# Sliding attention one unit at a time between the half tiles of a projection, with the gate recurrences beside its last tiles

## What is computed

```python
proj = h @ w_in[l]
q_a, k_a, v_a, q_m, k_m, v_m, o_m, i_m, f_m, g_a, g_m = jnp.split(proj, split_points, axis=-1)
...
y_a = sliding_window_attention(q_a, k_a, v_a, attn_sinks[l]).astype(x.dtype)

qk_m = jax.nn.silu(causal_depthwise_conv(jnp.concatenate([q_m, k_m], axis=-1), conv_w[l], conv_b[l]))
q_m, k_m = jnp.split(qk_m, 2, axis=-1)
i_pre = i_m + b_if[l][:MLSTM_HEADS]
f_pre = f_m + b_if[l][MLSTM_HEADS:]
h_m = mlstm_chunkwise(..., i_pre, f_pre)
y_m = (jax.nn.sigmoid(o_m.astype(jnp.float32)) * head_layer_norm(h_m, mlstm_norm_w[l])).astype(x.dtype)
merged = jax.nn.sigmoid(g_a) * (y_a @ w_branch_attn[l]) + jax.nn.sigmoid(g_m) * (y_m @ w_branch_mlstm[l])
```

## Time and profile before

| | us |
|---|---|
| median of 3 runs | 3319.88 |
| lowest and highest | 3318.41, 3323.91 |
| the profiled execution, its own time | 3337.6 |
| its span in the profile | 3335.7 |
| TensorE busy, share of the span | 3004.1, 90% |
| VectorE busy | 1268.3, 38% |
| ScalarE busy | 1017.8, 31% |
| GpSimd busy | 1001.5, 30% |
| mean granted clock of TensorE, share of full speed | 0.932 |

### The profile page before, as it was taken

The page is one execution under the profiler, slowest core; times in us unless marked ns, Lnnn a source line. Parts: engine busy times, 40 slices in busy tenths (PEclk is TensorE's granted clock), DMA queues, the critical chain, the costliest instruction groups (busy, mean ns, idle before and its releaser), DMA issues. The chain is left out here.

```text
span 3335.7 us, 38189 instructions
## 1 busy us (share of the span) xinstructions
PE 3004.1 (90%) x13920; PEld 2449.9 (73%) x13920; DVE 1268.3 (38%) x1998; ACT 1017.8 (31%) x1820; POOL 1001.5 (30%) x708
## 2 busy tenths in 40 slices
PE   3988966799899999999999788778989999998998
PEld 2876755566678888878888666667877888886877
DVE  6745235211152000001455886652436323333133
ACT  3223223100152000002444556524435212222243
POOL 2000311121263233224552122341035333332454
PEclk8987988899999999999999899885899999998999
DMA  5510200121241111113341122000034111111342
GB/s 189 179 59 0 63 13 0 38 57 38 79 142 57 50 50 44 50 37 120 123 130 45 39 64 88 26 13 1 0 101 139 32 50 48 47 50 56 102 142 92
DMA packets 191476, 221.46 MB, mean 66 GB/s; under 512 B 11145, under 2 KB 140297, under 8 KB 191369
## 3 DMA queue, kind: packets, MB, share of 16 engines
q1 hardware_dynamic: 191368, 220.05, 20.8%
HBM read 199.05 MB, written 20.97 MB: 66 GB/s over the span
## 5 line engine op out<-in xcount | busy, mean ns | idle before, releaser
L132 PE MATMUL psum<-sb_h_hi,sb_w_hi 128*128 128x512 f32 x1792 | 706.4, 394 | 13.8 <-POOL sb_w_lo L1038 9.2
L134 PE MATMUL psum<-sb_h_hi,sb_w_lo 128*128 128x512 f32 x1792 | 699.3, 390 | 0.0
L133 PE MATMUL psum<-sb_h_lo,sb_w_hi 128*128 128x512 f32 x1792 | 699.2, 390 | 0.0
L1424 POOL TENSOR_TENSOR sb_out_lo<-sb_out_raw,sb_out_hi 128x512 fp32r<-128x512 f32 (+1 forms) x180 | 323.3, 1803 | 410.4 <-ACT sb_out_hi L1414 410.3
L1036 POOL TENSOR_SCALAR sb_w_hi<-sb_w_raw 128x1024 fp32r<-128x1024 f32 x112 | 118.2, 1056 | 953.1 <-PE psum L134 676.1
L132 PEld LDWEIGHTS psum<-sb_h_hi,sb_w_hi 128*128 128x128 f32 x1792 | 337.6, 188 | 87.9 <-issue 13.4
L132 PE MATMUL psum<-sb_out_hi,sb_a_hi 128*128 128x512 f32 x960 | 382.3, 398 | 18.7 <-DVE sb_a_lo L1419 10.6
L133 PEld LDWEIGHTS psum<-sb_h_lo,sb_w_hi 128*128 128x128 f32 x1792 | 337.8, 189 | 73.4 <-issue 3.8
L134 PEld LDWEIGHTS psum<-sb_h_hi,sb_w_lo 128*128 128x128 f32 x1792 | 337.5, 188 | 70.5
L133 PE MATMUL psum<-sb_out_lo,sb_a_hi 128*128 128x512 f32 x960 | 378.3, 394 | 0.0
L134 PE MATMUL psum<-sb_out_hi,sb_a_lo 128*128 128x512 f32 x960 | 377.5, 393 | 0.0
(11 more groups left out here) (381 smaller groups left out, 4290.3 us busy)
## 6 DMA issues: line engine op xcount, KB each, us to landing
sb_w_raw<-in_w_up SPq DMA_DIRECT2D x44, 512.0 KB, 3.8
sb_late_w<-in_w_ada SPq DMA_DIRECT2D x32, 512.0 KB, 4.9
sb_w_raw<-in_w_in SPq DMA_DIRECT2D x56, 256.0 KB, 3.0
sb_w_raw<-in_w_in SPq DMA_DIRECT2D x28, 512.0 KB, 5.4
sb_w_raw<-in_w_ffn_gate SPq DMA_DIRECT2D x22, 512.0 KB, 3.8
sb_w_raw<-in_w_ffn_up SPq DMA_DIRECT2D x22, 512.0 KB, 3.9
sb_out_raw<-in_w_ffn_down SPq DMA_DIRECT2D x22, 512.0 KB, 3.6
sb_out_raw<-in_w_ffn_down SPq DMA_DIRECT2D x44, 256.0 KB, 3.0
```

What stands on the lines that cost most here:

```text
L132: nc.tensor.matmul(out, stationary.hi, moving.hi, start=start, stop=False)
L133: nc.tensor.matmul(out, stationary.hi, moving.lo, start=False, stop=False)
L134: return nc.tensor.matmul(out, stationary.lo, moving.hi, start=False, stop=stop)
L1424: self.nc.gpsimd.tensor_tensor(w.lo, raw, w.hi.bitcast(F32), ALU.subtract).then_inc(self.w_lo, 1)
```

## The change

The three blocks become one, which keeps the name `window_phase`. TensorE's stream is a straight list of 24 half tiles, numbered s; a half tile is 24 matmuls. The first 16 of them carry a unit each: the scores of unit s stand before half tile s, the transposes of unit s-1 after three of its eight feature blocks, the product with v of unit s-1 after six. Output rows are turned at odd s. The other engines' lists follow the same numbers. The convolution of a tile is given to VectorE in two parts, two taps in one step and one in the next. The gate work is a class, `Gates`: its inputs are turned in half tile 18, its results in half tile 23, its VectorE part stands at the end of VectorE's list, and its ScalarE parts stand between the sigmoids. The copies of the query block and key window are gone. The loops over tiles and query blocks are written out. Buffers have other places in SBUF, and `yaT` takes the place of `qT`, block by block.

```diff
+        @block.tensor
+        def _(pe):
+            def steps(s, first, last):
+
+                m, hf = s // 2, s % 2
+                if first == 0:
+                    if hf == 0:
+                        pe.wait_ge(split_done, m + 1)
+                    if m >= 2:
+                        if m - 2 < n_qk:
+                            pe.wait_ge(taps_done, m - 1)
+                        else:
+                            pe.wait_ge(o_done, m - 1 - n_qk)
+                for k in range(first, last):
+                    done = multiply(nc, core.ps[:, 2 * (m % 2) + hf, :], w[:, m % 2, k], h.half(k, hf), k == 0, k == KD - 1)
+                if last == KD:
+                    done.then_inc(mm_done, 1)
+
+            def scores(u):
+                n, g = u // 2, u % 2
+                if u:
+                    pe.wait_ge(s_read, u)
...
+            def turn(u):
+                pe.wait_ge(exp_done, 5 * u + 5)
+                if u:
+                    pe.wait_ge(o_read, u)
+                if u >= 2:
+                    pe.wait_ge(ya_out, u // 2)
...
+            def outputs(u):
+                n, g = u // 2, u % 2
+                pe.wait_ge(t_out_act, u + 1)
+                pe.wait_ge(t_out_dve, u + 1)
...
+            for s in range(2 * M):
+                if s < U:
+                    scores(s)
+                if s >= 3 and s % 2 and s <= U + 1:
+                    turn_outputs((s - 3) // 2)
+                steps(s, 0, 3)
+                if 1 <= s <= U:
+                    turn(s - 1)
+                steps(s, 3, 6)
+                if 1 <= s <= U:
+                    outputs(s - 1)
+                if s == U + 2:
+                    pe.wait_ge(ya_out, TB)
+                    gates.turn_in(pe)
+                if s == 2 * M - 1:
+                    gates.turn_out(pe)
+                steps(s, 6, KD)
...
+        @block.vector
...
+            for s in range(2 * n_qk + 2):
+                if s < U:
+                    maximum(s)
+                if 1 <= s <= U:
+                    turned_out(s - 1)
+                if s >= 2:
+                    conv(s // 2 - 1, (3,) if s % 2 else (1, 2))
+                if 1 <= s <= U:
+                    scaled(s - 1)
+            gates.rows(dve, chain)
+            gates.columns(dve, chain)
...
+        @block.scalar
...
+            for s in range(2 * n_qk + 3):
+                if 3 <= s <= U + 1 and s % 2:
+                    outputs((s - 3) // 2)
+                if 2 <= s <= 2 * n_qk and s % 2 == 0:
+                    base(s // 2 - 1)
+                if 1 <= s <= U:
+                    turned_out(s - 1)
+                if s < U:
+                    exponents(s)
+                if s >= 4 and s % 2 == 0:
+                    silu(s // 2 - 2)
+            act.wait_ge(silu_done, n_qk)
+            sigmoid(0)
+            gates.logs(act)
+            sigmoid(1)
+            gates.exps(act)
+            sigmoid(2)
+            sigmoid(3)
+            act.wait_ge(o_done, n_o)
```

More of the change, by code:

```diff
@@ L582, in _ @@
                 act.wait_ge(act_read, max(na, 1))
[L585 to L683, removed]
-                        nc.vector.tensor_copy(pT[:, g, 1], core.ps[:, 5, :]).then_inc(t_out_dve, 1)
-                        dve.wait_ge(exp_done, n * 10 + (5 * g + 5))
-                        chain(nc.vector.tensor_tensor(den[:, g], den[:, g], es[:, g], ALU.add))
-                        chain(nc.vector.reciprocal(part[:, g], den[:, g]))
-                        if more:
-                            maximum(n + 1, g)
-                        dve.wait_ge(pv_done, n * 2 + (g + 1))
-                        o = ob[:, 4 * g:4 * g + 4, :].rearrange("p (q a) e -> p a q e", q=2)
-                        src = core.ps[:, 6 + g, 0:4 * HD].rearrange("p (a q e) -> p a q e", a=2, q=2)
-                        r = part[:, g].rearrange("p (a q) -> p a q", a=2).unsqueeze(3).to_broadcast([P, 2, 2, HD])
-                        chain(nc.vector.tensor_tensor(o, src, r, ALU.mult))
-                        dve.sem_inc(o_free, 1)
-                    dve.sem_inc(o_ready, 1)
-                for g in range(2):
-                    maximum(0, g)
-                chain(nc.vector.tensor_copy(mask[:, 0:P], cst["band"]))
-                with dve.Fori(0, TB - 1) as n:
-                    chain.start(n, 12)
-                    round_(n, True)
-                    chain.end(TB - 1)
-                round_(TB - 1, False)
-            @block.scalar
-            def _(act):
-                act.sem_inc(t_out_act, 1)
-                act.sem_inc(ya_out, 1)
-                def exponents(n, g):
-                    act.wait_ge(neg_ready, n * 4 + (2 * g + 2))
-                    for j in range(4):
-                        nc.scalar.activation(pr[:, g, j], sc[:, g, j], ACT.Exp, bias=neg[:, g, j:j + 1],
-                                             accum_out=den[:, g, j:j + 1]).then_inc(exp_done, 1)
-                    nc.scalar.activation(es[:, g], sd[:, g], ACT.Exp).then_inc(exp_done, 1)
[L720 to L725, removed]
-                    act.wait_ge(ot_done, n + 1)
-                    nc.scalar.activation(yaT[:, :, bass.ds(n * P, P)], core.ps[:, 6, :].rearrange("p (j q) -> p j q", q=P),
-                                         ACT.Copy).then_inc(ya_out, 1)
-                for g in range(2):
-                    exponents(0, g)
-                with act.Fori(0, TB - 1) as n:
-                    round_(n, True)
-                round_(TB - 1, False)
-                act.wait_ge(ya_out, TB + 1)
@@ L826, in mlstm_phase @@
+def mlstm_phase(core, qmT, kmT, v_rows, R, gcol, dec, h_rows, cst, more_at):
     nc = core.nc
@@ L1122, in merge_phase @@
-def merge_phase(core, h, yaT, ymT, wv, wba, wbm, mT):
+def merge_phase(core, at, h, yaT, ymT, wv, wba, wbm, mT):
     nc = core.nc
```

400 lines of the change are left out of this document (230 added, 170 removed).

## The result

The changed kernel takes 3244.15 us (median of 4 runs, 3242.47 to 3248.81) against 3321.89 (4 runs, 3318.41 to 3331.66) for the one before, measured beside it: ratio 0.9764, 95% interval 0.974 to 0.9787. The forecast was 3236, with 3225 to 3272 as its range. The block itself, from its first instruction at 208.05 to the first one of mLSTM on GpSimd at 420.50, takes 212.4 us where the three stages took 298.8: 86.3 less, forecast 83.5.

A forecast was written before the change was run, and what follows sets the result against it. Attention and gates were taken as chains between engines, the projections as TensorE's own stream. The merged block's TensorE queue sums to 215.3 us against 298.8, 83.5 less; 3319.9 less that gives 3236, range 3225 to 3272.

The forecast's parts named there:

- Start (8.0): Block start: 8.0 us before the first tile's matmuls, until the first weights are there and split.
- Tiles (130.6): TensorE's queue: twelve projection tiles at 10.88 us each, 130.6 us.
- the slow first one (2.0): First tile: 2.0 us extra, since TensorE is idle before it.
- Units (65.8): Attention units in TensorE's queue: scores, transposes, products with v and output transposes, 65.8 us at the high clock.
- changes of kind (4.3): TensorE returning from small to large matmuls: 0.09 us each, three a step, 16 steps, 4.3 us; lower bound 0.
- Gates' transposes (2.9): Transposes of the gates on TensorE: 2.9 us at the high clock, from 5.7 at 0.59.
- End (1.7): Block end: last sigmoid 1.2 us after the last matmul, plus 0.5 for the barrier, 1.7 us.
- Margins: Hand-overs to TensorE: results ready early, by 1.1 us for VectorE's copy, 3.5 for the exponents, 3.5 for the gates.
- Table loads: ScalarE's queue: 20 loads where 14 were executed, six more, 7.7 us of ScalarE time, no term of the sum.
- B: Rival: short TensorE waits in each unit, and the clock falls with them; together 40 us, 3276; chance 0.19.
- C: Rival: small fp32 matmuls hold the low clock for the whole block; slower than before, 3440 at 0.5; chance 0.02.
- D: Rival: units overlap with large matmuls better than back to back; total under 3226; chance 0.02.

The follow-up runs named there:

- warm_start: Changed kernel plus twenty matmuls with unread results in the wait for the first weights: 3246.16 us, ratio 0.9746 to the kernel before.
- gates_behind: Changed kernel with the whole of the gates' work put behind the last tile: 3270.21 us, ratio 0.9813 to the kernel before.
- gates_later: Changed kernel with the gates' first transposes moved two half tiles on, their results not: 3246.62 us, ratio 0.9743 to the kernel before.
- after_again: Changed kernel, unchanged, profiled and timed again: 3236.51 us, ratio 0.973; its alternative: mLSTM takes 69 to 70 us again if the change caused it.
- wait_two: Changed kernel with the product right behind its transposes and VectorE's copy made three times: 3312.08 us, ratio 0.9934 to the kernel before.
- units_ahead: Changed kernel with all 16 units run before the first half tile, gates left in place: 3314.93 us, ratio 0.9961 to the kernel before.
- first_ahead: Changed kernel with the first tile's weights loaded and split at the end of the block before: 3229.02 us, ratio 0.9703 to the kernel before.

## Why the prediction was right

The step that the forecast rests on held: with the units between half tiles nothing in TensorE's queue waits behind the first weights, and its clock stays at 1.00, so the block is the sum of what the queue holds, 212.4 us against 215.3. Single terms were off, in both directions:

*Start (8.0).* 7.56 us from the first instruction to the first matmul of a tile.

*Tiles (130.6) and the slow first one (2.0).* In dense stretches the matmuls stand 0.226 to 0.227 apart, as in the earlier trace rows. The first tile was 2.3 us longer than warm_start's.

*Units (65.8) and changes of kind (4.3).* Both were off, in opposite directions. A unit between half tiles costs less than in the earlier trace rows: scores 1.06, transposes 0.80 in place of 0.99, product 1.70 in place of 1.83, output transposes 0.41 in place of 0.6. The matmuls around them cost more than forecast, 0.31 to 0.34 for the first behind a small one, with a longer last one ahead of the scores. Together two steps take 19.33 us (GpSimd's splits at 252.63 and 271.96) where the sum, changes of kind included, had 19.8. Over eight pairs that is 3.6 us less; with the start 0.4 less, the first tile 0.3 and the gates' transposes 0.7 more it makes 3.0, and the block came out 2.9 shorter than 215.3.

*Gates' transposes (2.9).* 3.6: 1.67 for the first (386.39 to 388.06) and 1.95 for the others (415.37 to 417.32), 0.7 too little. The working was wrong: 5.7 us at 0.59 are 3.4, and 2.9 is half of it, as if all of them had run at the low level. In the kernel before, the first sixteen took 1.91 us busy, the same as after, so they had the high one.

*End (1.7).* From the last matmul, about 418.8, to 420.50.

*Margins.* The copy as told: 1.19. The exponents of the step with a table load ended at 270.65, 8.8 us into it (forecast 8.9), and were wanted at 274.97; 4.3 were left in place of 3.5. The gates had 1.0 in place of 3.5, so that this margin and not the copy's was the narrowest. Their chain, 388.41 to 414.38, took 26.0 in place of the 23.7 of the earlier trace rows, and the cause is a resource that the prediction had left out. VectorE, then GpSimd:

```profile
396.46 3.46 DVE L639 SCALAR_TENSOR_TENSOR sb_logf<-sb_f_row,sb_abs_f 4x1024 f32<-4x1024 f32 x1 [3.51 <-ACT sb_abs_f L668]
399.96 2.28 DVE L640 TENSOR_TENSOR_SCAN sb_b_less_m<-sb_gate_lanes,sb_logf 4x1024 f32<-4x1024 f32 x1
```

```profile
396.46 2.39 POOL L1136 TENSOR_TENSOR sb_w_lo<-sb_w_raw,sb_w_hi 128x1024 fp32r<-128x1024 f32 x1
```

The VectorE instruction took 3.46 and ends 1.1 behind GpSimd's; in gates_behind and gates_later, where GpSimd had nothing to do beside it, it took 1.21. In the second profile of the changed kernel the same two start together again, and GpSimd is the one that waits, then VectorE's scan:

```profile
395.27 1.21 DVE L639 SCALAR_TENSOR_TENSOR sb_logf<-sb_f_row,sb_abs_f 4x1024 f32<-4x1024 f32 x1 [3.50 <-ACT sb_abs_f L668]
396.52 4.37 DVE L640 TENSOR_TENSOR_SCAN sb_b_less_m<-sb_gate_lanes,sb_logf 4x1024 f32<-4x1024 f32 x1
```

```profile
395.27 3.48 POOL L1136 TENSOR_TENSOR sb_w_lo<-sb_w_raw,sb_w_hi 128x1024 fp32r<-128x1024 f32 x1
```

One goes after the other, each as a whole: 2.1 to 2.3 us lost on VectorE either way. The Trainium skill states this ("SBUF — State Buffer", Who interferes with whom): a VectorE instruction with two inputs in SBUF and a GpSimd instruction that reads SBUF take turns on a shared pair of ports. The trace agrees. The prediction did not put it into the gates' margin, and it is nearly all of the 2.5 us by which that margin came out short.

*Table loads.* All 20 are there, each of 1.28, and they cost nothing on TensorE, as forecast. The 1.4 us more for a load that the prediction weighed did not appear: the load at 267.18 ended at 268.46, and the exponent behind it started at 268.48.

*The 8 us between 3236 and 3244.15* are not the block's, which was 2.9 shorter than forecast. 2.0 of them are the kernel before, 3321.89 beside the changed one where the forecast had started from 3319.9. The rest lies within what the clock of the later attention stage (16 us) moves between executions; no run ties it to a cause. In after_again the median was 3236.51, and that it meets 3236 so closely is luck.

*Rivals.* B did not come about, since no wait of its kind arose, but wait_two shows what stood 3.5 us away (the margin of 1.19 and a wait of 2.33): 283.5 us of block, most of the gain lost. C, the low clock through small matmuls, did not come about either; with the units by themselves (units_ahead) the clock was 0.61, between half tiles 1.00. The mechanism of D, units that overlap better with large matmuls, is there (3.6 us in the pairs), but too small for its time.

## What to carry to other kernels

When a serial stage is cut into the stream of the engine that bounds, ask of each hand-over how long before its use the result is ready, and treat the smallest margin as a threshold: here a wait of 0.9 us a step cost little more than its own length, one of 2.3 made the step 4.1 us longer, because the clock followed. Ask too what runs on the other engines beside a chain whose margin is small: one split of GpSimd took most of the gates' margin. Look through each in-order queue of the helpers for what stands behind a late instruction; in gates_later the tile's buffer was late before the result itself. And judge a change of a few us by the length of its stage in the profile, when another stage of the same kernel moves by 16.

## What the hardware showed beyond that

The later attention stage took 193 to 210 us with the same instructions, by the granted clock in its middle, and what chooses between them stayed open. The mLSTM stage, up to the first reduction of the norm behind it, took 65.6 to 69.6 us over the twelve profiles: 69.6 and 69.3 in the two of the changed kernel and 66.5 and 66.6 before it. By themselves these four fit the alternative set down for after_again, that the change costs 3 us there. But it took 68.1 in warm_start and 66.6 in first_ahead, which differ from the changed kernel only at the start of the block. Where low-clock stretches fall in it differs from profile to profile, and what sets that I can't say. The barrier between two blocks leaves TensorE idle for 1.4 us; behind it the first scores ran at the high level in five profiles and at the low one, wholly or for the most part, in five, and what decides is open.
